# A decoder layer on one core: the query projection of its routing as three float32r products of high and low halves, in place of float32 products

## What is computed

```python
x = layer_norm(ALPHA * x + (1.0 + g1) * mix, ln1_g[l], ln1_b[l])
h = x * (1.0 + sc2) + sh2                       # 512 x 2048
...
q = jnp.einsum('bsd,dhk->bshk', h, w_q).astype(jnp.float32)   # 2048 -> 8 heads x 128
s1 = jnp.einsum('bshk,nk->bshn', q[..., :half], sub_keys1.astype(jnp.float32))
s2 = jnp.einsum('bshk,nk->bshn', q[..., half:], sub_keys2.astype(jnp.float32))
v1, i1 = lax.top_k(s1, PEER_TOPK)
v2, i2 = lax.top_k(s2, PEER_TOPK)
```

## Time and profile before

| | us |
|---|---|
| median of 3 runs (lowest, highest) | 3253.71 (3250.67, 3255.66) |
| the profiled execution | 3245.96 |
| its span | 3244.2 |
| TensorE busy | 3109.5 (96%) |
| VectorE busy | 2455.2 (76%) |
| ScalarE busy | 1056.3 (33%) |
| GpSimd busy | 1026.5 (32%) |
| mean granted clock of TensorE in the span | 0.983 |

### The profile page before, as it was taken

How to read it: one execution, slowest core, us unless ns; L and a number is a source line. 1 busy time by engine, 2 the same in 40 slices (tenths; PEclk the granted TensorE clock), 3 DMA queues, 4 the chain that set the end, 5 groups by cost and what they waited for, 6 DMA issues and landing times.

```text
span 3244.2 us, 43813 instructions
## 1 busy us (share of the span) xinstructions
PE 3109.5 (96%) x16016; PEld 2659.8 (82%) x16016; DVE 2455.2 (76%) x3452; ACT 1056.3 (33%) x1632; POOL 1026.5 (32%) x734
## 2 busy tenths in 40 slices
PE   6999999999999999999999999999999999999994
PEld 4778887666469999997777899998999999999983
DVE  2397655645639999978888777888888888888757
ACT  1323545422223334332223333333333323333331
POOL 0110000000026553523222233435555554545200
PEclk9999999999999999999999999999999999999997
DMA  9786114465144555459888888888999899988853
GB/s 363 283 297 227 59 59 158 167 242 187 56 155 136 181 169 196 155 196 336 284 295 284 273 275 297 301 309 319 341 336 338 303 333 337 337 314 325 286 174 117
DMA packets 277725, 795.07 MB, mean 245 GB/s; under 512 B 118272, under 2 KB 138960, under 8 KB 230864
## 3 DMA queue, kind: packets, MB, share of 16 engines
q1 hardware_dynamic: 218816, 465.73, 42.6%
q0 software_dynamic: 50560, 317.87, 26.2%
q10 hardware_dynamic: 8208, 9.56, 0.8%
HBM read 750.07 MB, written 43.02 MB: 244 GB/s over the span
## 4 chain that ended last, share of the span: by engine, by line
PE 75%; DVE 18%; DMA 3%; issue 2%; ACT 1%; SPq 0%; POOL 0%; DVEq 0%; POOLq 0%; ACTq 0%
PE ps L2276 28%; PE ps L2212 26%; PE ps L1935 12%; DVE arena L1685 4%; PE ps L2187 3%; DVE arena L1682 2%; DMA arena<-in_w_ada 1%; DVE arena L1263 1%; PE ps L1959 1%; DVE arena L1710 1%; DVE split L1780 1%; PE ps L1894 1%; PE ps L1994 1%; PE ps L1871 1%; DVE win_parts L1250 1%
## 5 line engine op out<-in xcount | busy, mean ns | idle before, releaser
L2276 PE MATMUL ps<-split,w_parts 128*128 128x512 f32 x4608 | 1070.9, 392 | 20.0 <-DVE split L1780 17.2
L2276 PEld LDWEIGHTS ps<-split,w_parts 128*128 128x128 f32 x4608 | 863.8, 188 | 216.8 <-DVE split L1780 19.0
L2212 PE MATMUL ps<-h_parts,split 128*128 128x384 f32 x5376 | 947.4, 335 | 2.0 <-POOL split L788 1.4
L2212 PEld LDWEIGHTS ps<-h_parts,split 128*128 128x128 f32 x5376 | 933.7, 188 | 5.9 <-issue 1.6
L1125 ACT ACTIVATE split<-below_parts 128x1024 fp32r<-128x1024 f32 x416 | 441.7, 1062 | 1203.3 <-PE ps L2276 711.6
L1780 DVE TENSOR_TENSOR split<-below_parts,split 128x1024 fp32r<-128x1024 f32 x416 | 509.2, 1224 | 256.7 <-ACT split L1125 251.7
L800 POOL COPY arena<-arena 128x1 uint32 x256 | 209.8, 819 | 694.8 <-DVE arena L1734 389.4
L1715 DVE CUSTOM_DVE_ANT_0 arena<-arena 128x2048 f32<-128x2048 f32 x128 | 293.2, 2291 | 22.8 <-DMA arena<-in_u_tab,arena 22.8
L1734 DVE SCALAR_TENSOR_TENSOR arena<-arena 128x2048 f32<-128x2048 f32 x128 | 300.6, 2349 | 4.3 <-DVE arena L1726 2.2
L803 POOL DMA_INDIRECT arena<-in_v_tab,arena x128 | 257.4, 2011 | 104.4 <-POOL arena L800 103.1
L1250 DVE TENSOR_TENSOR win_parts<-arena,win_parts 128x512 fp32r<-128x512 f32 (+2 forms) x208 | 128.3, 629 | 210.5 <-ACT win_parts L854 201.3
(11 more groups left out here) (275 smaller groups left out, 3221.2 us busy)
## 6 DMA issues: line engine op xcount, KB each, us to landing
below_parts<-in_u_units SPq DMA_DIRECT2D x256, 512.0 KB, 4.7
below_parts<-in_v_tab SPq DMA_DIRECT2D x256, 512.0 KB, 6.9
arena<-in_w_ada SPq DMA_DIRECT2D x96, 1024.0 KB, 7.2
arena<-in_w_slices POOLq DMA_DIRECT2D x56, 512.0 KB, 4.6
gates_by_expert<-arena SPq DMA_DIRECT2D x24, 1024.0 KB, 4.8
below_parts<-gates_by_expert SPq DMA_DIRECT2D x32, 768.0 KB, 9.1
arena<-in_w_out POOLq DMA_DIRECT2D x32, 512.0 KB, 5.5
acts_ahead<-arena ACTq DMA_DIRECT2D x48, 192.0 KB, 2.1
```

The lines of the kernel that those rows point to most:

```text
L2212: ins = nc.tensor.matmul(ps[:, 6 + b, 0:DT], lhs[:, cols], h2_parts[:, rhs, k, :], start=k == 0 and n == 0, stop=k == KT - 1 and n == 2)
L2276: ins = nc.tensor.matmul(ps[:, g.bank_of(half, m) + b, :], w_parts[:, buf, lhs, i, m * P:(m + 1) * P], rhs[:, b * 512:(b + 1) * 512], star ...
```

## The change

Three new helpers and a new inner loop. `wq_high(k)` and `hq_high(k)` on ScalarE copy the weights of k (128x1024) and the input of k (128x512) into float32r tiles; `q_low(k)` on VectorE subtracts them from the originals into the second halves. TensorE waits for `wt_used`, which VectorE now raises behind each `q_low(k)`, and issues three products for each head. `wq_parts` has four slots (10K to 18K of the arena), `hq_parts` two (18K to 20K); both are given back through `q_used`. A weight slot of `wt` is free for its next load when VectorE has read it. Two semaphores are saved by counting `firsts_set` in `c_made` and `gate_row_ps` in `gate_row`.

```diff
--- before.py
+++ after.py
@@ -387,6 +387,10 @@
             y_high_att = early("y_high_att", [P, TB, 8, P], F32R)
             early("above_y", [P, YALOW - Q - 4 * K])
             y_low_att = early("y_low_att", [P, TB, 8, P], F32R)
+        with ExitStack() as first:
+            early("below_q", [P, Z])
+            wq_parts = early("wq_parts", [P, 4, 2, PH * P], F32R)
+            hq_parts = early("hq_parts", [P, 2, 2, S], F32R)
         y_high, y_low = [y_high_att, y_high_ssd], [y_low_att, y_low_ssd]
         assert XS == Z + 4 * K and Q == XS + 4 * K
 
@@ -565,7 +569,7 @@
...
             "sc_used pair_sub pair_exp topk_done row_used idx_copied dots_done gelu_done x1_moved h2_high h2_split parts_read "
...
         )
...
@@ -575,7 +579,7 @@
...
         wt_slot_full = [sem(f"wt_slot_full{i}") for i in range(4)]
         ring_full = [sem(f"ring_full{i}") for i in range(SLOTS)]
@@ -644,7 +648,7 @@
             sp.wait_ge(yn_low, 2 * TB)
             for slot in range(4):
                 weights(slot, w_q[slot, :, :])
-            sp.wait_ge(gate_row, 1)
+            sp.wait_ge(gate_row, 2)
             sp.dma_start(rows_out[:, :], gate_tile).then_inc(gate_stored, 16)
             sp.wait_ge(gate_stored, 16)
             for i, to in enumerate((sh2b, sc2b)):
@@ -979,7 +983,7 @@
                     nc.scalar.activation(cdec, alast, ACT.Exp)
                     nc.scalar.activation(dte, dte, ACT.Exp).then_inc(ssd_exp, 1)
                 if n == TURNED + 1:
-                    act.wait_ge(gate_row_ps, 1)
+                    act.wait_ge(gate_row, 1)
                     nc.scalar.activation(gate_tile, ps[0:3 * KT, 6, 0:P], ACT.Copy).then_inc(gate_row, 1)
                 if n == OUT:
                     act.wait_ge(proj_bank_free, placed(OUT - 1))
@@ -1055,9 +1059,24 @@
             mix_copy(UNITS - 1, DB)
             spread_root(1, TB + 1)
             spread_root(2, TB + 2)
+            def wq_high(k):
+
+                act.wait_ge(wt_slot_full[k % 4], 16 * (k // 4 + 1))
+                if k >= 4:
+                    act.wait_ge(q_used, k - 3)
+                nc.scalar.activation(wq_parts[:, k % 4, 0, :], wt[:, k % 4, :], ACT.Copy)
+
+            def hq_high(k):
+
+                if k >= 2:
+                    act.wait_ge(q_used, k - 1)
+                nc.scalar.activation(hq_parts[:, k % 2, 0, :], h2_t[:, k, :], ACT.Copy).then_inc(q_high, 1)
+
             for m in range(TB):
                 if m == 1:
                     spread_root(DB, TB + DB)
+                if m == DB:
+                    wq_high(0)
                 act.wait_ge(h2t_ps, m + 1)
                 for k in range(UPPER_FROM[m]):
                     ins = nc.scalar.activation(h2_t[:, k, m * P:(m + 1) * P], turned_block(m)[:, k, :], ACT.Identity,
@@ -1065,6 +1084,10 @@
                 ins.then_inc(h2t_ready, 1)
             act.wait_ge(h2t_ready, TB)
             act.wait_ge(h2t_upper, TB - 1)
+            hq_high(0)
+            for k in range(1, KT):
+                wq_high(k)
+                hq_high(k)
             act.wait_ge(x1_ready, TB)
             act.wait_ge(gate_stored, 16)
             nc.scalar.activation(h2_parts[:, 0, :, :], h2_t_dense, ACT.Copy).then_inc(h2_high, 1)
@@ -1187,7 +1210,7 @@
             dve.wait_ge(consts, 16)
             own(nc.vector.tensor_tensor(firsts[:, :], ident[:, 0:1], ident[:, 32:33], ALU.add))
             own(nc.vector.tensor_tensor(firsts[:, :], firsts[:, :], ident[:, 64:65], ALU.add))
-            nc.vector.tensor_tensor(firsts[:, :], firsts[:, :], ident[:, 96:97], ALU.add).then_inc(firsts_set, 1)
+            nc.vector.tensor_tensor(firsts[:, :], firsts[:, :], ident[:, 96:97], ALU.add).then_inc(c_made, 1)
 
             dve.wait_ge(small_loaded, 9 * 16)
             for m in (1, 4):
@@ -1593,16 +1616,31 @@
             upper(2)
             upper(3)
 
+            def q_low(k):
+
+                dve.wait_ge(q_high, k + 1)
+                nc.vector.tensor_tensor(wq_parts[:, k % 4, 1, :], wt[:, k % 4, :], wq_parts[:, k % 4, 0, :].bitcast(F32), ALU.subtract)
+                nc.vector.tensor_tensor(hq_parts[:, k % 2, 1, :], h2_t[:, k, :], hq_parts[:, k % 2, 0, :].bitcast(F32), ALU.subtract).then_inc(wt_used, 1)
+
+            dve.wait_ge(h2t_ready, TB)
+            q_low(0)
+            q_low(1)
             dve.wait_ge(ln1_loaded, 6 * 16)
             own(nc.vector.tensor_tensor(tmp2, ln1bb, sc2b, ALU.mult))
             own(nc.vector.tensor_tensor(sc2b, ln1gb, sc2b, ALU.mult))
+            q_low(2)
             own(nc.vector.tensor_tensor(sh2b, sh2b, tmp2, ALU.add))
             own(nc.vector.tensor_scalar(ln1gb, ln1gb, ALPHA, None, ALU.mult))
             own(nc.vector.tensor_scalar(ln1bb, ln1bb, ALPHA, None, ALU.mult))
-            own(nc.vector.tensor_tensor(h2_now, h2_now, sc2b, ALU.mult))
-            own(nc.vector.tensor_tensor(h2_now, h2_now, sh2b, ALU.add))
+            q_low(3)
             for m in range(TB):
                 affine(x1[:, m, :], m, x1[:, m, :], ln1gb, ln1bb).then_inc(x1_ready, 1)
+                q_low(4 + m)
+            own(nc.vector.tensor_tensor(h2_now, h2_now, sc2b, ALU.mult))
+            q_low(4 + TB)
+            own(nc.vector.tensor_tensor(h2_now, h2_now, sh2b, ALU.add))
+            for k in range(5 + TB, KT):
+                q_low(k)
 
             def best16(rows, step, used=None):
 
@@ -2136,13 +2174,13 @@
                         ins = nc.tensor.transpose(ps[:, 5, i * KT:(i + 1) * KT], ln1_tiles[:, i, :], ident[0:KT, 0:KT])
                     ins.then_inc(ln1_turned, 1)
                     pe.wait_ge(mod_ready, CHUNKS + MODS - 2)
-                    turn(ps[0:3 * KT, 6, 0:P], mod_cols[:, 3 * KT:6 * KT]).then_inc(gate_row_ps, 1)
+                    turn(ps[0:3 * KT, 6, 0:P], mod_cols[:, 3 * KT:6 * KT]).then_inc(gate_row, 1)
 
             pe.wait_ge(c_made, 2)
             chunk_part(0, 0)
             chunk_part(0, 1)
             pe.wait_ge(consts, 18)
-            pe.wait_ge(firsts_set, 1)
+            pe.wait_ge(c_made, 3)
             chunk_mod_sums(0)
             for n in range(LEFT):
                 unit_at(n)
@@ -2169,7 +2207,7 @@
             for m in range(TB):
                 pe.wait_ge(h2_ready, m + 1)
                 if m == 0:
-                    pe.wait_ge(gate_row, 1)
+                    pe.wait_ge(gate_row, 2)
                 if m == 1:
                     pe.wait_ge(mix_copied, 8 * TB)
                 if m >= 2:
@@ -2182,13 +2220,15 @@
             pe.wait_ge(h2t_ready, TB)
             pe.wait_ge(h2t_upper, TB - 1)
             for k in range(KT):
-                pe.wait_ge(wt_slot_full[k % 4], 16 * (k // 4 + 1))
+                pe.wait_ge(wt_used, k + 1)
                 for h in range(PH):
-                    ins = nc.tensor.matmul(bank(h), wt[:, k % 4, h * P:(h + 1) * P], h2_t[:, k, :], start=k == 0, stop=k == KT - 1)
+                    for n, (lhs, rhs) in enumerate(((0, 0), (0, 1), (1, 0))):
+                        ins = nc.tensor.matmul(bank(h), wq_parts[:, k % 4, lhs, h * P:(h + 1) * P], hq_parts[:, k % 2, rhs, :],
+                                               start=k == 0 and n == 0, stop=k == KT - 1 and n == 2)
                     if k == KT - 1:
                         ins.then_inc(q_ps, 1)
                 if k < KT - 1:
-                    ins.then_inc(wt_used, 1)
+                    ins.then_inc(q_used, 1)
             pe.wait_ge(key_loaded, 16)
             pe.wait_ge(q8_ready, PH)
```

More of the change, by code:

```diff
@@ L567, in decoder_layer @@
             "cols_ps cols_ready hot_ready g_ps g_staged pre_high pre_split pre_used pre_gelu high_done unit_split unit_used "
[L568 removed]
+            "tile_gelu w_made w_high w_ready v_read picks_w tail_loaded q_high gate_row gate_stored ada_row q_used x1_ready y_ready "
             "out_done var_ready root_ready"
@@ L577, in decoder_layer @@
          pre_high, pre_split, pre_used, pre_gelu, high_done, unit_split, unit_used, tile_gelu, w_made, w_high, w_ready, v_read,
-         picks_w, tail_loaded, gate_row_ps, gate_row, gate_stored, ada_row, firsts_set, x1_ready, y_ready, out_done, var_ready,
+         picks_w, tail_loaded, q_high, gate_row, gate_stored, ada_row, q_used, x1_ready, y_ready, out_done, var_ready,
          root_ready) = map(sem, names.split())
```

1 line of the change is left out of this document (removed).

## The result

The changed kernel took 3228.5 us (median of 7 runs, 3223.1 to 3240.5) against 3251.3 for the kernel before in the same comparison (7 runs, 3245.9 to 3265.3): a ratio of 0.993 with a 95% interval of 0.9908 to 0.9951, 16 to 30 us less. The prediction had 3236.7 us, 17.0 us less, in a range of 3230 to 3244. The direction is as forecast and 17 us lie inside the interval, but 3228.5 lies 1.5 us under the range. The profiled execution took 3231.8 us.

The account below looks back on a forecast made before the run. TensorE was taken as the bound in the query projection: 2.7 hand-off + 89.2 products + 2.9 stalls = 94.8 us against 111.8, 17.0 less, so 3253.7 - 17.0 = 3236.7 us, range 3230 to 3244.

Parts of the forecast that it names:

- The bound: Query projection: TensorE holds the stage for 111.8 us, and time saved there is saved for the program.
- The products: Query projection on TensorE: 384 float32r products at 0.228 us, 87.5 us in place of 111.8.
- The first hand-off: Start of the query projection: the first product waits 2.7 us for ScalarE's high half and VectorE's low halves.
- The first weights' half: ScalarE's high half of the k = 0 weights, between turned-input pieces: 1.06 us, costing nothing, at most 0.1 us.
- first product 5.7 us after the transposes: Sign at the query projection's start: its first product comes 5.7 us after TensorE's transposes.
- The cold start: First products of the query projection: 1.7 us lost to the lower clock, as in the kernel before.
- The gaps: Query projection, k = 5 to 7: TensorE waits for VectorE's low halves, 2.9 us in all (1.5 to 4.6).
- Loads and tail: Weight loads and x1 store cost nothing; at the end the 6144-wide low half has 1.2 us of cover, costing nothing.
- The stage's sum: Turned input to last product of the query projection: 2.7 + 89.2 + 2.9 = 94.8 us against 111.8.
- The range: Whole kernel: 3230 to 3244 us around 3236.7, with earlier runs taken to scatter by 3 us either side.
- Rivals: Four alternatives: clock lost in gaps 0.12, slower 0.04, slow feed or gain lost later 0.05, products not cheaper 0.01.
- Rival 1: Query projection: the clock falls at three late low halves, 5.1 us lost, gain 12 us, 3241.8 us; chance 0.12.

Follow-up runs that it names:

- before_third: The kernel before, unchanged, timed once more against itself for a further profile: ratio 0.9998 (0.9979 to 1.0016), stage 135.0 us.
- after_again: The changed kernel, unchanged, timed again against the kernel before: 3230.8 us (6 runs), ratio 0.9935 (0.9916 to 0.9954).
- after_third: The changed kernel, unchanged, timed once more against the kernel before: 3239.0 us (12 runs), ratio 0.9951 (0.9935 to 0.9967).

## Why the prediction was right, and where it was not

- **The bound.** Right: TensorE held the stage, and what was saved there stayed saved. The time between the first early unit and the first product of line 2276 is 506.5 to 507.1 us in all fourteen profiles.
- **The products.** Right at 0.228 us. The roughly 216 ns that the Trainium skill gives for an isolated product (TensorE: Matmul & The Clock Gate, "Back-to-back issue gap") would have given, as an estimate, 46.7 us for the 216 in one piece; they took 49.30.
- **The first hand-off.** 2.7 us forecast, 2.74 measured (821.55 to 824.29).
- **The first weights' half.** Wrong: "nothing, at most 0.1 us" was 0.94. I had taken ScalarE's idle time of 1.15 us from the earlier trace rows as a free place. But it was there only because TensorE's fourth block of transposes ran at the lower clock in that execution. In the three other profiles with the old stage that block took 1.97 us and ScalarE copied the last 20 pieces without a break, as here in before_third:

```profile
810.96 7.11 ACT L1063 ACTIVATE below_parts<-ps,h_shift,h_gain 128x128 f32<-128x128 f32 x20 [1.58 <-PE ps L1959]
```

In the changed kernel's profile the block took 1.97 us too, ScalarE's copies ended last, and a pass put among them moved the start. The shorter block and this pass are also why the sign "first product 5.7 us after the transposes" came as 8.05.
- **The cold start.** 1.7 us forecast. k = 0 took 8.59 us (824.29 to the release of hq_high(2) at 832.90) in place of 5.48: 3.1 us. In after_again the clock over the first 8 us was 0.77, not 0.62, so it was about 1.8 there. It differs between executions of one kernel, in the kernel before as well (0.62 to 0.82 in three profiles, 1.5 to 3.1 us).
- **The gaps.** Right in place and cause, and somewhat shorter: 2.4 us of delay for 2.9 (1.5 us of it stands as idle time in the rows). VectorE's turn is 6.39 us (848.44 to 854.83), not 6.6, since one pass starts before the one before it has ended. The cold start has no part in it: in after_again it cost 1.8 us in place of 3.0, and the gaps were 0.26, 0.65 and 0.65 us there.
- **Loads and tail.** Right: ScalarE waited for no load of weights, and the cover was 1.29 us.
- **The stage's sum.** 94.8 us from the turned input to the last product; measured 95.4 (821.55 to 916.95): the cold start 1.3 us over, the gaps 0.5 and the products 0.3 us under. The turned input itself was ready 0.7 us later, counted from the output projection, since the first weights' copy stood among its pieces. So the first profiles show 15.8 us saved (135.5 to 119.7) and the mean over all profiles 16.3, for 17.0.
- **The range.** This step failed: "the runs before scattered by 3 us to either side", with the level that it was put around. Three runs happened to lie within 5 us; 95 timed executions of the same kernel spread from 3240 to 3266. The stage's sum missed by 1.2 us; the point lay 8.2 us over the measured median, of which 2.4 are the level of the kernel before and 5.8 a difference of medians of 22.8 in place of 17.0. For the changed kernel the median of seven lay 6.6 us under the mean of its 25 executions. The twelve of after_third had a median of 3239.0, well inside the range: which side of 3230 a median of seven fell on was a matter of which executions they were. With 5 to 6 us to either side for the level, the range would have begun near 3228; that is said in hindsight. How much of the 22.8 us between the two medians is scatter and how much, if any, was saved outside the stage stays open, as above.
- **Rivals.** None came about in the stage. Rival 1 and the swinging clock that the Trainium skill describes (TensorE: Matmul & The Clock Gate, "A second HAM failure mode: psum-queue depth-cycling") didn't show: the granted clock was 1.00 through and behind the gaps of 0.26 to 0.65 us, in all five profiles that have them. But the argument against Rival 1, that a wait of 2.05 us ahead of the second scores left the clock at 1.00, held only for that one profile. In the changed kernel's the same wait is followed by 0.62 over 3 us:

```profile
921.79 3.14 PE L2241 MATMUL ps<-arena 64*128 64x128 f32 x32 [2.05 <-ACT arena L1104]
```

That is 3.14 us in place of 2.06. It was so in five of the fourteen profiles (0.50 to 0.64), with old stage and new. It cost nothing there: the first early unit starts 7.6 to 7.7 us after the first key score in all fourteen.

## What to carry to other kernels

A float32 product that stands on the critical path can be traded for three float32r ones where two other engines idle: here 0.87 us for 0.68 us, less an entry of about 3 us and the turns in which those engines have work of their own. Before a pass is called free because its engine idles there, ask what that idle time waited for; if it was an engine at a lowered clock, it need not be there in the next execution. And read how far a kernel's time scatters from more than three runs before drawing a range round a small gain.

## What the runs showed that I had not expected

The stage repeats to 1 to 3 us while the whole moves by 26 us between executions of one kernel. In the profiles the rest lies mostly ahead of the output projection's end (794.5 to 804.8 us) and in the late products (1751.6 to 1768.9 us), where it goes with ScalarE's wait for the loads of in_v_tab. With 32 transposes in the wait ahead of the projection, whose results nobody uses, the granted clock at its start was 1.00 in place of 0.71 and the products took 2.1 us less, in the one profile taken.
